# 768 transposes of an attention block with their operands typed fp32r in place of fp32, on one core

## What is computed

```python
h = _rmsnorm(x, norm_mix_g[l])
proj = h @ w_in[l]
...
o_a = _diff_attention(...)        # 4 heads, two softmax maps each: p0 - lam * p1
o_b = _chunk_band_attention(...)  # 8 heads, own and 8 previous chunks of 64
o_c = _forgetting_attention(...)  # 8 heads, causal, cumulative log-forget bias
...
merged = (g[:, :, 0] * (o_a @ w_br_a[l]) + g[:, :, 1] * (o_b @ w_br_b[l]) + g[:, :, 2] * (o_c @ w_br_c[l]))
x = x + merged @ w_out[l]
h = _rmsnorm(x, norm_ffn_g[l])
gt, up = jnp.split(h @ w_gate_up[l], 2, axis=-1)
x = x + (jax.nn.silu(gt) * up) @ w_down[l]
```

## Time and profile before

| | |
|---|---|
| median of 3 runs | 1825.85 us (1825.77 to 1826.04) |
| profiled execution | 1826.7 us, of which the span of the trace is 1824.9 us |
| TensorE busy | 1805.9 us (99%), 9048 matmuls |
| weight loads busy | 1519.5 us (83%) |
| VectorE, ScalarE, GpSimd busy | 1252.2, 898.3, 358.1 us |
| transposes of L1273 (probabilities) | 672, the first at 79.1 us, the last at 757.9 us |
| transposes of L1255 (V) | 96, from 72.2 to 706.2 us |

### The profile page before, as it was taken

How to read it: one execution, slowest core, us unless ns; L and a number is a source line. 1 busy time by engine, 2 the same in 40 slices (tenths; PEclk the granted TensorE clock), 3 DMA queues, 4 the chain that set the end, 5 groups by cost and what they waited for, 6 DMA issues and landing times. The chain is left out here.

```text
span 1824.9 us, 26104 instructions
## 1 busy us (share of the span) xinstructions
PE 1805.9 (99%) x9048; PEld 1519.5 (83%) x9048; DVE 1252.2 (69%) x2374; ACT 898.3 (49%) x1742; POOL 358.1 (20%) x350
## 2 busy tenths in 40 slices
PE   8999999999999999999999999999999999999998
PEld 6888888888888888888888888888888888888886
DVE  5467766667667766677655778787776877766675
ACT  5555655667666766653424224552333333344445
POOL 2356332112111121014220000002323232200011
PEclk9999999999999999999999999999999999999999
DMA  8526333222432234244236572225656576479522
GB/s 239 157 93 196 92 95 84 61 80 58 109 93 70 59 97 124 104 133 138 98 123 218 185 257 106 104 70 196 208 195 219 170 246 220 150 254 405 196 79 92
DMA packets 195946, 268.01 MB, mean 147 GB/s; under 512 B 9989, under 2 KB 132997, under 8 KB 191865
## 3 DMA queue, kind: packets, MB, share of 16 engines
q1 hardware_dynamic: 191944, 262.07, 43.6%
q0 software_dynamic: 1664, 4.19, 1.5%
q10 hardware_dynamic: 2224, 0.30, 0.1%
HBM read 187.82 MB, written 80.02 MB: 147 GB/s over the span
## 5 line engine op out<-in xcount | busy, mean ns | idle before, releaser
L220 PE MATMUL ps<-h_hi,w_hi 128*128 128x512 f32 x888 | 361.0, 407 | 2.6 <-DVE q_stack L1062 1.2
L222 PE MATMUL ps<-h_hi,w_lo 128*128 128x512 f32 x888 | 346.9, 391 | 0.0
L221 PE MATMUL ps<-h_lo,w_hi 128*128 128x512 f32 x888 | 346.8, 391 | 0.0
L855 POOL TENSOR_TENSOR w_lo<-w_raw,w_hi 128x256 fp32r<-128x256 f32 x148 | 109.3, 770 | 470.1 <-ACT w_hi L923 470.1
L222 PEld LDWEIGHTS ps<-h_hi,w_lo 128*128 128x128 f32 x888 | 166.7, 188 | 36.8
L220 PEld LDWEIGHTS ps<-h_hi,w_hi 128*128 128x128 f32 x888 | 167.2, 188 | 35.3 <-DVE q_stack L1062 2.4
L221 PEld LDWEIGHTS ps<-h_lo,w_hi 128*128 128x128 f32 x888 | 167.4, 188 | 28.9
L1091 DVE CUSTOM_DVE_ANT_0 probs_bc<-ps,bias 128x640 f32<-128x640 f32 (+7 forms) x128 | 90.4, 707 | 75.0 <-PE ps L1247 31.6
L2288 POOL TENSOR_TENSOR bias<-w_raw 128x512 f32<-128x512 f32 x19 | 26.8, 1409 | 517.2 <-PE ps L222 327.4
L220 PE MATMUL ps<-down_ring_w,down_ring_a 128*128 128x512 f32 x308 | 119.8, 389 | 0.0
L221 PE MATMUL ps<-down_ring_w,down_ring_a 128*128 128x512 f32 x308 | 119.8, 389 | 0.0
(11 more groups left out here) (367 smaller groups left out, 4435.1 us busy)
## 6 DMA issues: line engine op xcount, KB each, us to landing
w_raw<-in_w_in SPq DMA_DIRECT2D x50, 512.0 KB, 5.4
w_raw<-in_w_gate_up SPq DMA_DIRECT2D x44, 512.0 KB, 4.2
k_stack<-k_stack SPq DMA_DIRECT2D x24, 512.0 KB, 5.4
gate_in<-gates_scratch SPq DMA_DIRECT2D x24, 512.0 KB, 3.7
down_rows<-in_w_down SPq DMA_DIRECT2D x11, 1024.0 KB, 7.1
hidden_scratch<-hidden_stage SPq DMA_DIRECT2D x22, 512.0 KB, 4.8
weight_sums_scratch<-weight_sums SPq DMA_DIRECT2D x11, 1024.0 KB, 4.9
gates_scratch<-gate_sigmoid SPq DMA_DIRECT2D x21, 512.0 KB, 2.6
```

Source lines behind the costliest of these rows:

```text
L220: nc.tensor.matmul(out, w_hi, x_hi, start=first, stop=False)
L221: nc.tensor.matmul(out, w_hi, x_lo, start=False, stop=False)
L222: return nc.tensor.matmul(out, w_lo, x_hi, start=False, stop=last)
L855: last = nc.gpsimd.tensor_tensor(w_lo[part], w_raw[part], w_hi[part].bitcast(F32), ALU.subtract)
```

## The change

Two more names are given to places in SBUF, both typed fp32r: `probs_words`, 4 x 1024 words per partition at the place where both `probs_a` and `probs_bc` begin, and `v_words`, 1024 words at the place of `v_fm`. The transposes of turn_v and turn_probs take their data through these names, take `ident_r` in its own type, and write to a view of the turn bank typed fp32r. Nothing else is changed: what writes the probabilities and V still writes them as fp32 through the old names, and what reads the turn banks reads them as before. No instruction is moved on any engine.

```diff
         also = lambda name, shape, dt, begins: nc.alloc_sbuf_tensor_at(name, shape, dt, offset=begins)
+        probs_words = also("probs_words", [P, 4, T], F32R, 178176)
+        v_words = also("v_words", [P, T], F32R, 83968)
@@ turn_v
                     for j in range(4):
-                        last = nc.tensor.transpose(turn_bank[lc % 2][:, j * P:(j + 1) * P],
-                                                   v_fm[:, (4 * lc + j) * P:(4 * lc + j + 1) * P], ident[:, :])
+                        last = nc.tensor.transpose(turn_bank[lc % 2][:, j * P:(j + 1) * P].bitcast(F32R),
+                                                   v_words[:, (4 * lc + j) * P:(4 * lc + j + 1) * P], keep["ident_r"][:, :])
@@ turn_probs
                     pe.wait_ge(mixed, c["outs"] + (i + 1))
-                    src = probs_a[:, 2 * (i % 2), :]
+                    src = probs_words[:, 2 * (i % 2), :]
                 else:
                     pe.wait_ge(scaled[s % 2], STEPS // 2 * (c["unit"] - UPB) + (s // 2 + 1))
-                    src = probs_of(b, s)
+                    src = probs_words[:, s % 3, :]
@@
                     for x in range(size):
-                        last = nc.tensor.transpose(turn_bank[lc % 2][:, x * P:(x + 1) * P],
-                                                   src[:, tile * P:(tile + 1) * P], ident[:, :])
+                        last = nc.tensor.transpose(turn_bank[lc % 2][:, x * P:(x + 1) * P].bitcast(F32R),
+                                                   src[:, tile * P:(tile + 1) * P], keep["ident_r"][:, :])
```

## The result

The changed kernel takes 1816.02 us (median of 5 runs, 1815.77 to 1817.18), the kernel before it beside it 1825.85 (1825.61 to 1826.04). The ratio is 0.9947 with a 95% interval of 0.9934 to 0.9961: 9.8 us or 0.54% faster. The forecast was 1811 in a range of 1793 to 1828; the sign is right, and the gain is two thirds of the 14.5 us that were forecast. The profiled execution took 1817.2 us, its span is 1815.4.

A forecast was written before the change was run, and what follows sets the result against it. The prediction took TensorE as the bound. It saved 16.1 us inside transpose runs, lost a tenth, and took the remaining 14.5 us from 1826.7 to 1812.2, or 1811 us against the median; range 1793 to 1828.

The forecast's parts named there:

- TensorE is the bound in attention: Attention: TensorE busy 681.6 of 686 us, so time taken from its stream comes off the span.
- Units of load and stream before the change: TensorE: fp32 transposes load in one unit (some 55 ns), stream in two; ordinary fp32r matmuls the other way round.
- The distance: Inside transpose runs: starts 82 ns apart instead of 109, load and stream at one and a half units each.
- The test by the load's length: Next profile's transpose loads: 140 ns long would mean one unit, 188 two, telling the cases apart.
- a rule against itself: Transposes: SBUF latency dominates their some 275 ns, so halving array work gains next to nothing; time as with no change.
- The sum: Inside the 172 transpose runs: 596 distances, each falling from 109 to 82 ns, save 16.1 us.
- A tenth lost: Attention: some earlier starts end waiting for ScalarE and VectorE to free a turn bank, leaving 14.5 us of gain.
- What is late next: Attention: the forgetting branch's score read, where VectorE waits for TensorE and would wait less; no size given.
- no change: Rival on the transposes: distance stays 108 or 109 ns, 1825 us; chance 0.31.
- a slower kernel: Rival inside runs: fp32r transpose load and stream do not overlap, distance 165 ns, 1868 us; chance 0.15.
- The whole gain: Rival inside runs: load and stream take one unit each, 31.0 us saved before losses, 1797 us; chance 0.24.

The follow-up runs named there:

- x1: Changed kernel with all 768 transposes made as ordinary fp32r matmuls with the rounded identity, on tiles of h_hi: 1830.02 us, 14.0 slower than the changed kernel.
- x3: Changed kernel with branch C's 128-column diagonal mask matmul placed between the two score matmuls instead of last: 1816.79 us.
- x7: Changed kernel with each unit's eight V transposes placed one by one between the matmuls of the next two projection pieces: 1833.74 us, 17.7 more.
- x8: Changed kernel with 96 transposes of the two later blocks and 64 of the first also fp32r, GpSimd writing the rounded identity early: 1817.04 us.
- x10: x8 with twelve more fp32 transposes of the identity in a first-block wait: two runs at 1814.09 and 1814.46 us, three at 1816.41 to 1816.80.
- x9: Changed kernel with the unbroken V transpose run behind all four projection pieces instead of the first two: 1838.69 us, 22.7 more.

## Why the prediction came out as it did

- **TensorE is the bound in attention, and what its stream loses comes off the span**: right. Attention became 10 us shorter with TensorE at 99% of it, and the later stretch stayed within a microsecond.
- **Units of load and stream before the change**: right, and x1 bears out the two-unit load of fp32r outside the transpose mode (loads of 192 ns, distance 111).
- **The distance, 82 ns between bounds of 57 and 109**: it is 84 by the loads of the V group and 85 by all loads. The number was right, the reason given for it was not, so that it came within 2 ns is luck: the load and the stream do not take one and a half units each. The load is usable after one unit, the stream takes one, and only the distance between loads is one and a half. The test by the load's length, 140 ns for one unit and 188 for two, does not tell the cases here: the load is 140 ns long although the loads are what sets the pace. The Trainium skill, "TensorE: Matmul & The Clock Gate", section "Weight-path perf modes — Fast Weight Load (FWL) and DoubleRow", has the fast load on for 128 weights of any type but FP32. If that is meant to cover fp32r, it is not borne out in these runs: the fp32r loads are 84 or 108 ns apart, the fp32 ones can be 57. The figure of the Trainium skill on that page, Part 4: PE-mode transpose, about 275 ns in a kernel's context, is for bf16; it fits the 273 ns of the fp32 ones before, but a shorter stream did gain time, which speaks against the conclusion that the prediction drew from it as a rule against itself.
- **The sum, 16.1 us inside the runs**: at 25 ns (109 less 84) it is 596 x 25 = 14.9 us. That error is 1 us.
- **A tenth lost**: this is the term that was mis-sized. Of 14.9 us, 9.8 arrived, so a third was lost, not a tenth. Both kernels have the same 9048 matmuls in the same order, so the traces can be laid side by side. Over the 172 runs the time from first start to the second matmul behind sums to 126.1 us before and 114.9 after: 11.2 us, so 3.7 are lost at and in the runs. Half of that (1.87 of 3.69 us) is in the 56 runs of branch C with the 128-column mask matmul right ahead, an edge to which the prediction gives no price: the first fp32r transpose's load keeps the next one away for 84 ns and the 57 ns stream ahead hides only part of it. x3 took 1.3 us of this away, at the cost of more elsewhere; the other 0.6 us is in part waits as in the next sentences.

  Another 0.96 us is in eight runs of branch B behind a 320-column matmul, which lose 87 to 160 ns each. In four of them the projection matmul right behind the transposes waits longer for VectorE's evacuation of the projection (before, then after):

```profile
327.73 0.50 PE L220 MATMUL ps<-h_hi,w_hi 128*128 128x512 f32 x1 [0.15 <-DVE q_stack L1062]
...
323.34 0.50 PE L220 MATMUL ps<-h_hi,w_hi 128*128 128x512 f32 x1 [0.37 <-DVE q_stack L1064]
```

  Three runs of branch C end in the same wait. All seven together, before and after:

```profile
PE ps L220 <- DVE q_stack L1062: 1.2, 7, 0.2
...
PE ps L220 <- DVE q_stack L1064: 2.4, 7, 0.4
```

  In the other four the first load waits until VectorE has emptied the turn bank, a wait that the profile of before does not show, and two distances inside the run are 115 to 131 ns:

```profile
329.20 0.56 PEld L1275 LDWEIGHTS ps<-ident_r,probs_words 128*128 128x128 f32 x5 [0.25 <-DVE probs_tb_lo L1114]
```

  The remaining 0.86 us is spread over the other runs. Between 11.2 us and the 9.8 of the medians (9.5 between the profiled executions) lies what was lost outside the runs: attention's other stretches are 1.3 us longer together, the blocks before and behind it 0.4. The 1.3 is a balance: two waits for the mixed map went away (1.5 us less), one wait for ScalarE's scaled probabilities grew by 0.45 us, and many first loads of a run wait some 0.1 us longer. So the mechanism named for the lost tenth, earlier starts that end in a wait, is there; the short cover of a load is the part that the prediction lacks.
- **What is late next**: the score read of branch C was named, where VectorE would wait less. It did, a little: 69.5 us before and 66.8 after for the scores of branches B and C together, before and after:

```profile
DVE probs_bc L1091 <- PE ps L1247: 31.6, 36, 2.4
DVE probs_bc L1091 <- PE ps L1245: 25.9, 27, 1.7
DVE probs_bc L1091 <- PE ps L1273: 12.0, 10, 1.8
...
DVE probs_bc L1093 <- PE ps L1275: 31.4, 30, 1.8
DVE probs_bc L1093 <- PE ps L1249: 29.6, 29, 2.5
DVE probs_bc L1093 <- PE ps L1247: 5.8, 7, 1.5
```

  The row of the transposes grew from 12.0 to 31.4 and that of the scores of L1247 (L1245 before) shrank from 25.9 to 5.8; together they went from 37.9 to 37.2, so the waits only stand under another line. VectorE did not become a bound.
- **A number of the prediction**: the 7384 rows that it gives TensorE stand in no view; nothing hangs on them.
- **The rivals**: no change and a slower kernel are out by the interval, and x1 shows what the former was about: the two-unit load belongs to fp32r outside the transpose mode. The slower case, loads that do not overlap with streams, is seen nowhere. The whole gain did not come, because the loads stand 84 ns apart and not 57.

## What to carry to other kernels

A transpose of four-byte words in a run costs 109 ns typed fp32, 84 typed fp32r, and 111 as an ordinary fp32r matmul with the identity. The gain is in the distances inside a run, n - 1 of n: a lone transpose gains nothing (0.12 us either way, by x7 and by the runs of one, 347 ns before and 342 after to the second matmul behind), and a 128-column matmul right ahead takes some of it back, because the load is then uncovered (runs of one there are 18 to 20 ns longer than before). Count runs, not instructions, and look at what stands at their edges. Here a third of the gain was lost, with two other engines in rings behind TensorE and two banks between. Before transposes are moved, look at what their consumers' queues hold behind them: V's run 2.5 to 2.8 us later cost 18 to 23 us, a third of the latter by the clock, and one piece earlier gave nothing.

## What was not expected of the hardware

- Loads of fp32r transposes are 84 to 88 ns apart although each is as long in the profile (140 ns) and usable as early (57 ns) as an fp32 one, whose successor can follow at 57.
- In the first block, TensorE's granted clock fell to 1.2 GHz for 6.8 us in x8 and for 3.4 us in x10 and in x9, whose first block is unchanged. In the 2 us before, TensorE had been busy for 0.82, all and 0.78 of the time. The falls cost 2.85 us in x8 and 1.5 in x9. The changed kernel, as little busy between 16 and 18 us (1.01 of 2.00 us) as x8, had none.
